# Adding every gathered value row on TensorE in 64x64 tiles, without the running sum on VectorE

## What is computed

```python
# for each block of 128 tokens; 8 heads, 16 picks per head = 128 picks per token
q = (xb @ w_pq).reshape(128, 8, 2, 128)
s = einsum("thpd,hpkd->thpk", q, sub_keys)          # scores against 2 x 128 sub keys
...                                                  # top 16 of each side, top 16 of their sums
g   = softmax(best_s)
ue  = take(u, idx)                                   # 128 rows of 1024 per token
act = gelu(einsum("thkd,td->thk", ue, xb))
ve  = take(v, idx)                                   # 128 rows of 1024 per token
out = einsum("thk,thkd->td", g * act, ve)
```

## Time and profile before

| | |
|---|---|
| time, median of 3 runs | 4110.6 us (4108.55 to 4118.33) |
| span of the profiled execution | 4121.6 us (no time of its own is given beside it) |
| PE matmul busy | 3236.2 us, 79% |
| DVE busy | 2740.1 us, 66% |
| ACT busy | 1361.8 us, 33% |
| POOL busy | 1326.5 us, 32% |
| read from memory | 1188.19 MB, 1073.81 MB of it by the gathers |
| mean granted TensorE clock | 0.910 |

### The profile page before, as it was taken

How to read it: one execution, slowest core, us unless ns; L and a number is a source line. 1 busy time by engine, 2 the same in 40 slices (tenths; PEclk the granted TensorE clock), 3 DMA queues, 4 the chain that set the end, 5 groups by cost and what they waited for, 6 DMA issues and landing times. The chain is left out here.

```text
span 4121.6 us, 38098 instructions
## 1 busy us (share of the span) xinstructions
PE 3236.2 (79%) x9308; PEld 1596.0 (39%) x9308; DVE 2740.1 (66%) x5542; ACT 1361.8 (33%) x3634; POOL 1326.5 (32%) x1194
## 2 busy tenths in 40 slices
PE   6888799867898798898999879956665765655676
PEld 2444478633444344443445634422222222222222
DVE  3556542655788687874676657768877886886666
ACT  1222340323444444442343323333332332333332
POOL 0100000002344343332333234435444444554443
PEclk8999999888899898999999999979997898898888
DMA  2100222426888787876899899989999998998998
GB/s 73 34 29 28 67 87 77 142 75 268 310 325 314 290 324 291 311 299 252 347 355 363 323 369 401 398 364 421 421 404 371 421 414 364 421 420 359 422 421 365
DMA packets 197686, 1209.58 MB, mean 293 GB/s; under 512 B 21328, under 2 KB 33744, under 8 KB 65360
## 3 DMA queue, kind: packets, MB, share of 16 engines
q0 software_dynamic: 147456, 1073.81, 64.9%
q1 hardware_dynamic: 44672, 113.26, 7.9%
q10 hardware_dynamic: 5328, 20.08, 1.3%
HBM read 1188.19 MB, written 18.87 MB: 293 GB/s over the span
## 5 line engine op out<-in xcount | busy, mean ns | idle before, releaser
L1658 PE MATMUL bank<-peer_ring,peer_diag 128*128 128x512 f32 x3072 | 1590.1, 661 | 571.2 <-ACT peer_diag L1639 569.9
L1545 POOL DMA_INDIRECT peer_ring<-in_uv,peer_index x1024 | 1244.4, 1215 | 1762.2 <-PE bank L1658 1088.2
L1558 DVE CUSTOM_DVE_ANT_0 peer_ring<-peer_ring,peer_xn 128x1024 f32<-128x1024 f32 x1024 | 1246.1, 1221 | 585.8 <-DMA peer_ring<-in_uv,peer_index 544.4
L1658 PEld LDWEIGHTS bank<-peer_ring,peer_diag 128*128 128x128 f32 x3072 | 601.3, 208 | 1468.8 <-ACT peer_diag L1639 881.6
L1632 ACT ACTIVATE peer_coefs<-peer_dots 128x1 f32<-128x1 f32 x1024 | 205.7, 201 | 1461.7 <-DVE peer_dots L1558 1460.0
L1583 DVE SCALAR_TENSOR_TENSOR peer_vsum<-peer_ring,peer_coefs,peer_vsum 128x1024 f32<-128x1024 f32 x248 | 317.6, 1281 | 21.6 <-ACT peer_coefs L1634 21.6
L1639 ACT ACTIVATE peer_diag<-ident,peer_coefs 128x128 f32<-128x128 f32 x768 | 308.5, 402 | 67.9 <-PE bank L1658 5.1
L1634 ACT ACTIVATE peer_coefs<-peer_coefs,peer_gates 128x1 f32<-128x1 f32 x1024 | 301.5, 294 | 33.3
L689 DVE SCALAR_TENSOR_TENSOR q_acc<-q1mixers_hT,q1mixers_w_tap,q_acc 128x512 f32 x216 | 162.0, 750 | 4.6 <-issue 0.6
L689 DVE SCALAR_TENSOR_TENSOR q_acc<-q0mixers_hT,q0mixers_w_tap,q_acc 128x512 f32 x200 | 150.4, 752 | 6.8
L494 PE MATMUL bank<-q_aT,q1mixers_w_vg 128*128 128x512 f32 x256 | 119.4, 613 | 18.2 <-DMA q1mixers_w_vg<-in_w_vg 14.6
(11 more groups left out here) (272 smaller groups left out, 3513.1 us busy)
## 6 DMA issues: line engine op xcount, KB each, us to landing
q0mix_w<-in_w_mix SPq DMA_DIRECT2D x40, 512.0 KB, 3.6
q1mix_w<-in_w_mix SPq DMA_DIRECT2D x40, 512.0 KB, 6.7
peer_ring<-in_uv,peer_index POOLq DMA_INDIRECT x1024, 11.6
q0mixers_w_vg<-in_w_vg SPq DMA_DIRECT2D x16, 512.0 KB, 3.5
q0scores_w<-in_w_peer SPq DMA_DIRECT2D x16, 512.0 KB, 3.7
q1mixers_w_vg<-in_w_vg SPq DMA_DIRECT2D x16, 512.0 KB, 8.0
q1scores_w<-in_w_peer SPq DMA_DIRECT2D x16, 512.0 KB, 13.8
peer_sc<-sc_dram ACTq DMA_DIRECT2D x6, 1024.0 KB, 9.5
```

The costliest lines, as they stand in the source:

```text
L1545: pool.indirect_dma_start(out=p.ring[:, r, :], out_offset=None, in_=p.c.dram["uv"], in_offset=bass.IndirectOffsetOnAxis(ap=p.index[:, n:n ...
L1558: dve.tensor_tensor_reduce(row, row, p.xn[:, :], 1.0, 0.0, ALU.mult, ALU.add, p.dots[:, n:n + 1]).then_inc(p.dotted, 1)
L1658: mm = pe.matmul(p.c.bank[:, 6 + h, :], p.diag[:, m % p.DIAGS, :], p.ring[:, r, D + h * C:D + (h + 1) * C], start=(n == 0), stop=(m == p.P ...
```

## The change

All 128 picks of a block are added on PE. The diagonal matrix is kept in two pieces of 64x64: tokens 0 to 63 and 64 to 127 stand on their own partitions, in a buffer of 128x64 (ACT scales `ident_half`, two identities of 64 one under the other). PE multiplies in four tiles per pick: token half t (partitions 64t and up, into bank 6 + t) and column half h (output partitions 64h and up), each 64 rows by 64 columns by 512. `close` gathers the result from the banks in four pieces of 64 partitions. `vsum`, its semaphores and the operations on it are gone. A semaphore increment stands between PE's wait for the diagonal and the matmuls.

```diff
-        self.diag = sb("diag", [P, self.DIAGS, P])
+        self.diag = sb("diag", [P, self.DIAGS, HALF])
...
     def wait_used(self, eng, b, n):
-        if self.by_vector(n):
-            eng.wait_ge(self.added_v, self.V_PICKS * (b + 1) + self.v_place(n) + 1)
-        else:
-            eng.wait_ge(self.added, self.PE_PICKS * (b + 1) + self.pe_place(n) + 1)
+        eng.wait_ge(self.added, PICKS * (b + 1) + n + 1)
...
     def dot(self, n):
-        if n >= self.LAG:
-            self.add_here(n - self.LAG)
...
     def close(self):
-        for n in range(PICKS - self.LAG, PICKS):
-            self.add_here(n)
         dve.wait_ge(p.h1_in, 16 * (b + 1))
-        dve.wait_ge(p.added_v, p.V_PICKS * (b + 2))
-        dve.tensor_tensor(p.h1[:, :], p.h1[:, :], p.vsum[:, :], ALU.add).then_inc(p.vsum_ready, 1)
-        dve.wait_ge(p.vsum_ready, b + 2)
-        dve.wait_ge(p.added, p.PE_PICKS * (b + 2))
+        dve.wait_ge(p.added, PICKS * (b + 2))
         for h in range(2):
             cols = slice(h * C, (h + 1) * C)
-            dve.tensor_tensor(p.h1[:, cols], p.h1[:, cols], p.c.bank[:, 6 + h, :], ALU.add).then_inc(p.summed, 1)
+            for t in range(2):
+                tok = slice(t * HALF, (t + 1) * HALF)
+                dve.tensor_tensor(p.h1[tok, cols], p.h1[tok, cols], p.c.bank[h * HALF:(h + 1) * HALF, 6 + t, :],
+                                  ALU.add).then_inc(p.summed, 1)
...
     def gelu(self, n):
-        if not p.by_vector(n):
-            m = p.pe_place(n)
-            act.wait_ge(p.coef_ready, PICKS * (b + 1) + n + 1)
-            act.wait_ge(p.added, p.PE_PICKS * (b + 1) + m + 1 - p.DIAGS)
-            act.activation(p.diag[:, m % p.DIAGS, :], p.c.ident[:, :], ACT.Copy, scale=coef).then_inc(p.diag_ready, 1)
+        act.wait_ge(p.coef_ready, PICKS * (b + 1) + n + 1)
+        act.wait_ge(p.added, PICKS * (b + 1) + n + 1 - p.DIAGS)
+        act.activation(p.diag[:, n % p.DIAGS, :], p.c.ident_half[:, :], ACT.Copy, scale=coef).then_inc(p.diag_ready, 1)
...
     def add(self, n):
-        if p.by_vector(n):
-            return
-        m = p.pe_place(n)
         if n == 0:
             pe.wait_ge(p.ms_ready, 2 * b + 1 + 1)
-        pe.wait_ge(p.diag_ready, p.PE_PICKS * (b + 1) + m + 1)
+        pe.wait_ge(p.diag_ready, PICKS * (b + 1) + n + 1)
+        pe.sem_inc(self.p.c.passed, 1)
         for h in range(2):
-            mm = pe.matmul(p.c.bank[:, 6 + h, :], p.diag[:, m % p.DIAGS, :], p.ring[:, r, D + h * C:D + (h + 1) * C],
-                           start=(n == 0), stop=(m == p.PE_PICKS - 1))
+            for t in range(2):
+                tok = slice(t * HALF, (t + 1) * HALF)
+                mm = pe.matmul(p.c.bank[h * HALF:(h + 1) * HALF, 6 + t, :], p.diag[tok, n % p.DIAGS, :],
+                               p.ring[tok, r, D + h * C:D + (h + 1) * C], start=(n == 0), stop=(n == PICKS - 1))
         mm.then_inc(p.added, 1)
```

More of the change, by code:

```diff
@@ L61 @@
 LOWEST = -3e38
+HALF = P // 2
 HR = 3
@@ L193, in _ @@
             pool.memset(ones[:, :], 1.0).then_inc(cst, 1)
-            pool.wait_ge(cst, 3)
+            pool.memset(c.ident_half[:, :], 0.0).then_inc(cst, 1)
+            pool.wait_ge(cst, 4)
             pool.affine_select(out=ident[:, :], in_=ident[:, :], compare_op=ALU.not_equal, fill=1.0,
@@ L199, in _ @@
                                base=0, pattern=[[-1, P]], channel_multiplier=1).then_inc(cst, 1)
+            for n, base in enumerate((0, -HALF)):
+                if n:
+                    pool.wait_ge(cst, 7)
+                pool.affine_select(out=c.ident_half[:, :], in_=c.ident_half[:, :], compare_op=ALU.not_equal, fill=1.0,
+                                   base=base, pattern=[[-1, HALF]], channel_multiplier=1).then_inc(cst, 1)
         groups = [KT, N_CQ, N_CKV]
@@ L245, in _ @@
             if q == 0:
-                pe.wait_ge(cst, 5)
+                pe.wait_ge(cst, 8)
             def sums(g):
@@ L1297 @@
     DIAGS = 4
-    SPAN, OF_VECTOR = 4, (3,)
-    V_PICKS = PICKS // SPAN * len(OF_VECTOR)
-    PE_PICKS = PICKS - V_PICKS
     def __init__(self, c, ctx):
@@ L1348, in rows_buffers @@
         self.h1 = sb("h1", [P, D])
-        self.vsum = sb("vsum", [P, D])
         self.g_final = sb("g_final", [P, D])
-        self.diag = sb("diag", [P, self.DIAGS, P])
+        self.diag = sb("diag", [P, self.DIAGS, HALF])
         self.dots = sb("dots", [P, PICKS])
@@ L1357, in rows_buffers @@
         self.root = sb("root", [P, 1])
-    BEFORE = {"tensor": [("added", PE_PICKS)], "scalar": [("gelued", PICKS), ("coef_ready", PICKS), ("diag_ready", PE_PICKS), ("exp_done", 1), ("root_ready", 1)],
+    BEFORE = {"tensor": [("added", PICKS)], "scalar": [("gelued", PICKS), ("coef_ready", PICKS), ("diag_ready", PICKS), ("exp_done", 1), ("root_ready", 1)],
               "vector": [("dotted", PICKS),
-                         ("added_v", V_PICKS), ("vsum_ready", 1), ("gates_set", 1), ("routed", ROUTE), ("summed", 2),
+                         ("gates_set", 1), ("routed", ROUTE), ("summed", 4),
                          ("ms_ready", 2), ("inv_ready", 1), ("y_ready", 1)],
@@ L1371, in before @@
                          "ms_ready": self.ms_ready, "inv_ready": self.inv_ready, "y_ready": self.y_ready,
[L1372 to L1384, removed]
+                         "index_set": self.index_set, "coef_ready": self.coef_ready}[s_], n)
     def wait_used(self, eng, b, n):
-        if self.by_vector(n):
-            eng.wait_ge(self.added_v, self.V_PICKS * (b + 1) + self.v_place(n) + 1)
-        else:
-            eng.wait_ge(self.added, self.PE_PICKS * (b + 1) + self.pe_place(n) + 1)
+        eng.wait_ge(self.added, PICKS * (b + 1) + n + 1)
     def route(self, dve, b, fed=None):
@@ L1502 @@
     AHEAD = {"pool": 3, "tensor": -5, "scalar": -1, "vector": 0}
-    LAG = 2
     ROUTE_FROM = 4
@@ L1568, in dot @@
                 self.done += 1
-    def add_here(self, n):
-        p, dve, b = self.p, self.eng, self.b
-        if not p.by_vector(n):
-            return
[L1575 to L1585, removed]
     def close(self):
         p, dve, b = self.p, self.eng, self.b
-        for n in range(PICKS - self.LAG, PICKS):
-            self.add_here(n)
         dve.wait_ge(p.h1_in, 16 * (b + 1))
-        dve.wait_ge(p.added_v, p.V_PICKS * (b + 2))
-        dve.tensor_tensor(p.h1[:, :], p.h1[:, :], p.vsum[:, :], ALU.add).then_inc(p.vsum_ready, 1)
-        dve.wait_ge(p.vsum_ready, b + 2)
-        dve.wait_ge(p.added, p.PE_PICKS * (b + 2))
+        dve.wait_ge(p.added, PICKS * (b + 2))
         for h in range(2):
             cols = slice(h * C, (h + 1) * C)
-            dve.tensor_tensor(p.h1[:, cols], p.h1[:, cols], p.c.bank[:, 6 + h, :], ALU.add).then_inc(p.summed, 1)
-        dve.wait_ge(p.summed, 2 * (b + 2))
+            for t in range(2):
+                tok = slice(t * HALF, (t + 1) * HALF)
+                dve.tensor_tensor(p.h1[tok, cols], p.h1[tok, cols], p.c.bank[h * HALF:(h + 1) * HALF, 6 + t, :],
+                                  ALU.add).then_inc(p.summed, 1)
+        dve.wait_ge(p.summed, 4 * (b + 2))
         squares = p.c.bank[:, 6:8, :].rearrange("p a n -> p (a n)")
@@ L1627, in gelu @@
         if n == 0:
-            act.wait_ge(p.added_v, p.V_PICKS * (b + 1))
             act.wait_ge(p.gates_set, b + 2)
@@ L1705, in build @@
         c.ident = sb("ident", [P, P])
+        c.ident_half = sb("ident_half", [P, HALF])
         c.ones = sb("ones", [P, P])
```

3 lines of the change are left out of this document (removed).

## The result

The changed kernel takes 4236.68 us (median of 4 runs, 4224.06 to 4240.4) against 4113.12 us in the same rounds: a ratio of 1.0293, 95% interval 1.0259 to 1.0326. It is slower by 3%, where 3970 us, faster by 3.5%, had been forecast.

What follows compares the result with a forecast made beforehand. PE was taken to fill the time in blocks 0 to 2, DMA nearly in 3 and in 4 to 7. -138 and -7 made -145 on 4121.6 us: 3977, about 3966 as measured, rounded up to 3970; range 3925 to 4390.

Steps and rivals of the forecast that it cites:

- PE's cost per pick: In busy stretches, four tiles side by side take 0.90 us per pick instead of 1.72; 115 us per block for 165.
- No overlap: Rival: tiles never run side by side, 3.43 us per pick, 5680 us in all; chance 0.06.
- the case in between: Rival: unhidden loads or a wait for the shared bank, 1.2 us a pick, 4090 us in all; chance 0.13.
- The order rival: Rival on PE's adds: 1.72 us per pick with tiles, 4350 us in all; chance 0.33.
- The price of a switch: On PE, a turn into the small form and back costs 0.29 us; 18 us each in blocks 0 and 1.
- The sum for blocks 0 to 3: -32 us each in blocks 0 and 1, -43 in 2, -15 in 3, plus less PE waiting for DVE: -138 together.
- The 8 us that were booked as a gain from DVE: In blocks 0 and 1, DVE's 41 us less work cuts PE's waits for DVE by some 8 us each.
- I take 0: ACT's tighter wait for a free diagonal buffer costs nothing; from above, 56 us in block 0.
- Blocks 2 and 3: Block 2 saves 50 us less 7 for switches, -43; block 3 is held by DMA to -15.
- The end: Closing sums after the last block take 4.05 us instead of 3.96: no difference.
- the forecast's own range: Whole kernel 3920 to 4060 us: from switches that cost nothing up to 1.1 us per pick.
- Blocks 4 to 7: DMA hides PE's work inside these blocks; only their starts gain, -1.7 us each, -7 in all.

Runs made afterwards that it cites:

- the tiles alone: Kernel before with 64x64 tiles for PE's three picks of four, DVE keeping every fourth pick and vsum: 4109.22 us, ratio 0.9967.
- at four behind: Changed kernel with PE's adds written four picks behind DVE instead of five: 4059.56 us, ratio 0.9856.
- three picks behind: Changed kernel with PE's adds written three picks after DVE instead of five: 4077.07 us, ratio 0.9898.
- 8 buffers: Changed kernel with eight diagonal buffers instead of four, nothing else: 4229.67 us, ratio 1.0282.
- the later release alone, on DVE: Kernel before with DVE's addition of every fourth pick five picks late instead of two (LAG = 5): 4571.89 us, ratio 1.1112.
- with full matmuls: Changed kernel with full 128x128 matmuls instead of tiles for all picks on PE, and eight diagonal buffers: 4336.64 us, ratio 1.0541.

## Why the prediction was wrong

**PE's cost per pick: right.** 0.90 us was taken, 0.88 was measured. No overlap (3.43) and the case in between (1.2) are refuted: four halves start every 0.43 us, and seven picks take 6.17 us. The order rival, which the chances give 0.33 and up to which the range reaches, was an estimate of the author's, 1.72 us per pick and 4350 us in all; no run shows that price for tiles, and the runs showed 0.88 us in its place.

**The price of a switch: right.** 0.29 us per turn was read off; two picks between full matmuls took 5.51 us against 5.52 by the sum.

**The sum for blocks 0 to 3: wrong, in the step "In blocks 0 to 2 PE is what fills the time".** From there 50 us of saved PE time less 18 for switches was booked as 32 us off blocks 0 and 1 each. They got 65 and 72 us longer. PE's busy time was no bound there: with the tiles alone, PE was busy for 30 and 41 us less and the blocks did not get shorter (485 and 489 for 478 and 485). The same paragraph held the right reading, "there the gathers follow PE", but took it as a matter of how long PE works, when it was one of when, in the written order, the add of a pick stands.

**What was not costed: DVE's share as a release.** The prediction priced the removed additions as 41 us of work per block and let 8 of them count. That every fourth slot came free at two picks behind the dot, and would now come free at five, stands in its description of the kernel and in no term of the sum. At five behind, three of eight picks are left to issue a gather, land it and be ready: at block 0's old pace 3 x 478 / 128 = 11.2 us, at its new one 3 x 543 / 128 = 12.7 us. The trace has, from a gather's issue to its landing in block 0, first in the kernel before and then in the changed kernel at four behind:

```profile
DMA to landing us min/median/max: 5.3/8.4/20.0
...
DMA to landing us min/median/max: 5.8/8.6/17.2
```

With 8.4 us of 11.2 gone in the middle case, little is left for POOL's issue and for uneven steps; a fourth pick makes it 14.9 at the old pace. This is an estimate that fits. (So is the 12 us for a gather and its neighbours in the expectation for three picks behind: 8.4 us to landing and 1.09 for POOL's issue, both medians of block 0 before, and 1.2 for the dot make 10.7.) What is shown is that one pick's distance moves 177 us, and that the dots of block 0 that had to wait for a row go from 35 before to 61 in the changed kernel and to 33 at four behind. The 8 us that were booked as a gain from DVE in each of blocks 0 and 1 had the wrong sign too: PE's wait for DVE grew from 20 to 68 us.

**ACT: effect right, size of the wait wrong.** "I take 0" holds for the time (8 buffers: 4230 against 4237), though the wait grew from 1.9 to 125 us in block 0, more than twice the upper end of 56.

**Blocks 2 and 3: sign right, too large.** -20 and -4 us instead of -43 and -15.

**Two smaller slips.** The end was put at 4.05 us; from ACT's last diagonal to the end of the bank sums it took 5.45, as PE's eight halves took 2.02 us and not some 1.1. And 1.1 us per pick by the terms given makes 3966 + 3 x 26 = 4044, not the 4060 of the forecast's own range.

**Blocks 4 to 7: right in kind.** No pace was lost. At the start of block 6 the first gather left 3.16 us after the first add began, for 4.59 in the earlier trace rows:

```profile
3575.06 7.58 PE L1599 MATMUL bank<-peer_ring,peer_diag 64*64 64x512 f32 x48 [24.00 <-ACT peer_diag L1580]
3578.22 1.06 POOL L1510 DMA_INDIRECT peer_ring<-in_uv,peer_index  x1 [25.40 <-PE bank L1599]
```

That is 1.4 us less, with 1.7 expected. The 1.7 was an estimate, the difference of four full halves and two steps of tiles at a granted clock of 0.50. At that clock full halves started 0.86 and 0.85 us apart in the kernel before (weight loads at 3462.36, 3463.22 and 3464.07 us), and groups of four halves of tiles 0.86 and 0.85 us apart in the changed one (3576.79, 3577.65 and 3578.50 us); at the start itself no run shows 1.7 us, and the trace has 1.4. Over the four blocks this is lost among differences of up to 6 us between single blocks.

**What stays open.** How the loss in blocks 0 and 1 divides between the later release of every fourth slot and the rest of what left with DVE's share was not measured apart: the later release alone, on DVE, cost 32 and 44 us there, but it also delays DVE's own order. Writing PE's adds earlier moves two things at once, the release of the slots and the place of the adds among PE's own jobs; with DVE's share kept, the same step from five to four behind moved the place just as much and blocks 0 and 1 went from 485 and 489 to 482 and 502, so the place by itself does not bring the gain. No run with more slots in the ring at five behind tested the release apart. Why one pick earlier is enough, and why the step from four to three brings 16 us in block 0 and 5 in block 1, is not settled either, nor what does set the length of blocks 0 and 1 in the kernel before, where neither less work on PE nor earlier rows shortened them. That the low clock was no cause rests on three runs: with tiles alone it fell to 0.84 and 0.85 and the blocks kept their length, with full matmuls it was near 0.90 and the blocks stayed long, and at four behind it returned when the waits went.

## What to carry to other kernels

An operation in a ring of buffers has two outputs, its result and the free slot; before moving it to another engine, look at when the slot comes free in the new engine's written order, and count what is left for the next transfer against how long a transfer takes. An engine at 87% busy is not the bound for that alone: test it by making its work shorter with the order kept, as the run with tiles alone did, and then retune the distances between the engines before judging the change. A long new wait in the profile (125 us here) may cost nothing, while a shift of one pick in the written order was worth 177 us.

## What the runs showed of the hardware

Float32 matmuls in four 64x64 tiles ran four at a time: four halves of 512 columns started every 0.43 us, where one full-width half did. The loads of 64 columns, four in 0.15 us, went with them at the same spacing of 0.43 us. A turn from full to 64-row matmuls and back cost 0.29 us, one to tiles and back 0.32 (5.51 less 3.43 and 2 x 0.88). PE did the adds of the blocks that run alone at a granted clock of 0.66 to 0.69 on average, against 0.84 to 0.90 before, and these blocks took 1359 us for 1361, with the DMA engines 93 to 101% busy.
